# A mixture-of-experts block in front of a second mixer: output shares added in another order, router rows kept in natural order, a key norm moved up, and empty expert rows skipped by the gathers' bound

## The reference, cut to what matters

```python
# first block
x = x + diff_attention(rmsnorm(x, norm_mix), ...)
h = rmsnorm(x, norm_ffn)
logit_g = h @ w_group + b_group                 # 4 groups
logit_e = h @ w_router + b_router               # 16 experts
# each token: the best group, in it the best two of four experts, two weights
x = x + sum over the two experts of weight * (silu(h @ w_gate[e]) * (h @ w_up[e])) @ w_down[e]
# second block
xn = rmsnorm(x, norm_g) * (1 + sc_x) + sh_x
f_in, f_gate, q, k, v, na_gate = split(xn @ w_in)
q, k = rmsnorm(heads(q)), rmsnorm(heads(k))     # likewise keys and values of 256 context rows
mix = concat(fourier(f_in) * silu(f_gate), neighbourhood_attention(q, k, v, ...) * silu(na_gate))
x = x + g_x * (mix @ w_out)
```

## Time and profile before

| | us |
|---|---|
| median of 3 runs | 910.46 (909.38 to 911.85) |
| profiled execution, whole time | 911.67 |
| its span in the trace | 909.9 |
| PE busy | 890.8 (98%) |
| DVE, ACT, POOL busy | 377.2, 214.8, 177.5 |

### The profile page before, as it was taken

One profiled execution on the slowest core, in us unless ns is written; L12 is line 12 of the kernel. 1 busy time (PEld: TensorE's weight loads), 2 busy tenths in 40 slices (PEclk: granted clock), 3 DMA queues, 4 the chain that ended last, 5 costly groups with the idle time before them and its releaser, 6 DMA issues.

```text
span 909.9 us, 13423 instructions
## 1 busy us (share of the span) xinstructions
PE 890.8 (98%) x5562; PEld 505.1 (56%) x5562; DVE 377.2 (41%) x810; ACT 214.8 (24%) x469; POOL 177.5 (20%) x164
## 2 busy tenths in 40 slices
PE   9999999999999989999999999999999999999997
PEld 5588875455564433333333333344688888856553
DVE  2765442457755453310310210047635542454355
ACT  2211213345544210010110110124201111633320
POOL 3211220000003054230320200033202203290001
PEclk9999999999999999999999999999999999999999
DMA  9945559024011978999999999961382102700002
GB/s 326 322 112 186 185 207 390 29 93 185 1 47 52 277 197 329 412 415 426 423 422 428 421 429 428 402 234 47 110 173 100 42 15 79 246 1 2 1 1 92
DMA packets 71470, 188.47 MB, mean 207 GB/s; under 512 B 31201, under 2 KB 31857, under 8 KB 65137
## 3 DMA queue, kind: packets, MB, share of 16 engines
q1 hardware_dynamic: 62432, 162.41, 48.7%
q0 software_dynamic: 5488, 18.37, 5.4%
q10 hardware_dynamic: 3488, 6.82, 2.0%
HBM read 168.70 MB, written 18.89 MB: 206 GB/s over the span
## 4 chain that ended last, share of the span: by engine, by line
PE 81%; DMA 7%; DVE 5%; ACT 2%; POOL 2%; issue 2%; SPq 0%; DVEq 0%; ACTq 0%; POOLq 0%
PE psum L974 20%; PE psum L1178 14%; PE psum L1199 8%; PE psum L882 6%; PE psum L1076 5%; DMA ring<-in_moe_w_up 5%; PE psum L1024 4%; PE psum L1001 4%; PE psum L1329 2%; PE psum L1038 2%; PE psum L1055 2%; PE psum L1449 2%; PE psum L1398 2%; PE psum L1103 2%; PE psum L1291 2%
## 5 line engine op out<-in xcount | busy, mean ns | idle before, releaser
L1178 PE MATMUL psum<-ring,buf_a 128*32 128x512 f32 x1536 | 168.5, 597 | 3.8 <-issue 2.8
L1178 PEld LDWEIGHTS psum<-ring,buf_a 128*32 128x32 f32 x1536 | 53.5, 111 | 115.2 <-issue 115.2
L1199 PE MATMUL psum<-ring,buf_c 128*32 128x512 f32 x768 | 84.1, 593 | 0.0
L2712 POOL DMA_INDIRECT buf_b<-xq_d,o_sb x48 | 51.6, 1075 | 158.2 <-DVE buf_a L2296 126.1
L2319 DVE TENSOR_TENSOR buf_c<-buf_c,psum 128x512 f32<-128x512 f32 x12 | 13.1, 1089 | 154.4 <-PE psum L1178 154.4
L2639 POOL TENSOR_TENSOR qk_st<-qk_st,half 128x8 f32<-128x8 f32 x26 | 43.6, 1677 | 158.6 <-DVE qk_st L2378 72.9
L974 PE MATMUL psum<-ring,buf_a 128*128 128x256 f32 x320 | 70.9, 380 | 0.0
L974 PE MATMUL psum<-ring,buf_b 128*128 128x256 f32 x288 | 64.8, 380 | 0.0
L974 PEld LDWEIGHTS psum<-ring,buf_a 128*128 128x128 f32 x320 | 60.1, 190 | 8.2 <-issue 0.4
L1946 DVE TENSOR_TENSOR s_buf<-s_buf,psum 128x512 f32<-128x512 f32 x52 | 35.3, 685 | 61.2 <-PE psum L974 57.3
L974 PEld LDWEIGHTS psum<-ring,buf_b 128*128 128x128 f32 x288 | 53.9, 190 | 7.5 <-issue 0.6
(11 more groups left out here) (322 smaller groups left out, 1239.2 us busy)
## 6 DMA issues: line engine op xcount, KB each, us to landing
ring<-in_moe_w_gate SPq DMA_DIRECT2D x16, 2048.0 KB, 15.1
ring<-in_moe_w_up SPq DMA_DIRECT2D x16, 2048.0 KB, 16.0
ring<-in_moe_w_down SPq DMA_DIRECT2D x16, 2048.0 KB, 15.4
ring<-in_w_in SPq DMA_DIRECT2D x7, 2048.0 KB, 14.3
ring<-in_w_ada SPq DMA_DIRECT2D x6, 2048.0 KB, 9.7
ring<-in_da_w_in SPq DMA_DIRECT2D x5, 2048.0 KB, 15.8
y_d<-ring POOLq DMA_DIRECT2D x1, 5632.0 KB, 22.2
y_d<-buf_b ACTq DMA_DIRECT2D x11, 512.0 KB, 12.2
```

The costliest lines, as they stand in the source:

```text
L1178: last = mm(buf("mm", n)[rows, :], x_part[:, j, k, :], slot(moe_load(q, m, r))[:, k, :], start=(k == 0), stop=(k == KD - 1))
L1199: last = mm(buf("sc", n)[rows, m, :], hidT[:, s % 3, f * P + SUB * j:f * P + SUB * (j + 1)], slot(moe_load(q, 2, r), FC)[:, f, m * CH:(m + ...
L2712: pool.indirect_dma_start(out=xg[:, s % 2, j * 256:(j + 1) * 256], out_offset=None, in_=xn_quarters, in_offset=bass.IndirectOffsetOnAxis(a ...
```

## The change

- `xs2` is written in the order of `x`; PE's transposes read every eighth column of it, and `x_turn` reads the gathered rows so. `xn_d` and its four stores are gone; `xq_d` is stored with one DMA for a tile, those of the first three tiles ahead of SP's load of the sixth matrix.
- The token numbers in `slot_pick` are lowered by 4096 and 4*4096 is added back in `quarter`, so that a slot without a token has an index beyond the table. The gathers are given a bound, beyond which a row is not fetched.
- The places of tokens beyond 96 (`spill_places`) are worked out later, with the `picks` step among the experts' steps.
- The first key norm, j=CT, is moved ahead of the last tile's third norm on DVE and POOL, in parts.
- The output shares: every product is added straight from PSUM to each quarter of `x` that it belongs to (13 additions of a quarter and two of half a quarter, all on DVE, none on ACT or POOL); the order of the products and of the stores is another, and one mix sum is made earlier.

```diff
+NO_ROW = 8 * SEQ
+    out_bank |= {"P3": out_bank["P1"], "P7": out_bank["P5"], "P6": out_bank["P2"]}
@@ SP
+        def store_rows(t):
+            sp.wait_ge(xs2_ready, t + 1)
+            sp.dma_start(xq_d[t * P:(t + 1) * P, :], xs2[:, t, :]).then_inc(xq_stored, 16)
         for i in [0, 1, 4, 2, 5, 3, *range(SLOTS, len(order))]:
...
             elif i == 3:
-                for t in range(TT):
-                    sp.wait_ge(xs2_ready, t + 1)
-                    for n in range(4):
-                        sp.dma_start(xq_d[t * P:(t + 1) * P, n * 256:(n + 1) * 256].rearrange("p (k a) -> p k a", k=KD),
-                                     xs2[:, t, :].rearrange("p (k q a) -> p k q a", k=KD, q=4)[:, :, n, :]
-                                     ).then_inc(xq_stored, 16)
+                store_rows(TT - 1)
                 filled(sp, "sc", turn["sc", "cv"])
...
             load(moe_load(q, m, r), matrix(m, 4 * q + r), FC if m == 2 else KD)
+            if i == 2:
+                for t in range(TT - 1):
+                    store_rows(t)
...
-        for ready, t, a in ((1, 0, 0), (1, 1, 0), (2, 2, 0), (2, 3, 0), (0, 2, 1), (0, 3, 1), (3, 0, 1), (4, 1, 1)):
+        for added, t, a in ((5, 0, 0), (5, 1, 0), (11, 2, 0), (11, 3, 0), (12, 2, 1), (12, 3, 1), (13, 0, 1), (13, 1, 1)):
+            sp.wait_ge(out_added, added)
+            if added == 13:
+                sp.wait_ge(out_ready, t + 1)
@@ PE
+        def xs2_rows(t, k):
+            return xs2[:, t, :].rearrange("p (q k) -> p k q", k=KD)[:, k]
-                        transposes(n, [xs2[:, t, k * P:(k + 1) * P] for t in range(TT - 1)])
+                        transposes(n, [xs2_rows(t, k) for t in range(TT - 1)])
...
         out_seventh("S3", "T3", out_bank["P5"])
-        pe.wait_ge(s_out_ready, 2)
+        pe.wait_ge(s_out_ready, 3)
+        pe.wait_ge(out_added, 4)
+        out_seventh("S2", "T2", out_bank["P3"])
+        pe.wait_ge(out_added, 7)
+        out_seventh("A22", "T4", out_bank["P7"])
         out_seventh("S1", "T1", out_bank["P4"])
...
         pe.wait_ge(s_out_ready, 4)
-        pe.wait_ge(out_added, 6)
-        out_seventh("S4", "B22", out_bank["P4"])
+        out_seventh("S4", "B22", out_bank["P6"])
@@ DVE
+        link(V.tensor_scalar(quarter[:], quarter[:], 4.0 * NO_ROW, None, ALU.add))
-                V.tensor_scalar(xs2[:, t, :].rearrange("p (k q) -> p q k", k=KD),
-                                x[:, t, :].rearrange("p (q k) -> p q k", k=KD),
-                                rstd[:, 4 + t:5 + t], None, ALU.mult).then_inc(xs2_ready, 1)
+                V.tensor_scalar(xs2[:, t, :], x[:, t, :], rstd[:, 4 + t:5 + t], None, ALU.mult).then_inc(xs2_ready, 1)
-                            tok_f[:, t:t + 1], ALU.is_equal, ALU.mult).then_inc(pick_ready, 1)
+                            tok_below[:, t:t + 1], ALU.is_equal, ALU.mult).then_inc(pick_ready, 1)
-            V.transpose(xsT[:, s % 4, :], xg[:, s % 2, :]).then_inc(x_turned, 1)
+            V.transpose(xsT[:, s % 4, :].rearrange("p (j k a) -> p j k a", j=4, k=KD),
+                        xg[:, s % 2, :].rearrange("p (j a k) -> p j k a", j=4, k=KD)).then_inc(x_turned, 1)
             elif name == "picks":
+                spill_places()
                 last_picks()
...
         add_last(3)
-        norm3_mean(3)
-        norm3(3)
         for t in range(TT):
...
             qk_mean(CT + t)
+            if t == 0:
+                norm3_mean(3)
             qk_scale_unit(CT + t)
+            if t == 0:
+                norm3(3)
...
+        dve.wait_ge(mix_ready, TT)
+        mix_sum(3)
         add_out_f(turn["sc", "out_f", TT - 1], TT - 1)
-        dve.wait_ge(mix_ready, TT)
-        for n in (3, 1, 2, 4):
+        for n in (1, 2, 4):
             mix_sum(n)
...
# the additions in their new order, waits left out:
# x11 x12 x21 x22 of P1; x11 of P2; x21 x22 of P5; x21 x22 x12 of P3;
# x21 of P7; x22 x12 of P4; then the two halves of x12 of P6
@@ POOL
-            for t in tiles:
-                pool.wait_ge(xs2_ready, t + 1)
-                pool.dma_start(xn_d[t * P:(t + 1) * P, :], xs2[:, t, :]).then_inc(xn_stored, 16)
-        pool.wait_ge(xn_stored, TT * 16)
...
-                                        in_offset=bass.IndirectOffsetOnAxis(ap=idx[:, 4 * s + j:4 * s + j + 1], axis=0)
+                                        in_offset=bass.IndirectOffsetOnAxis(ap=idx[:, 4 * s + j:4 * s + j + 1], axis=0),
+                                        bounds_check=4 * SEQ - 1, oob_is_err=False
...
         norm3_power(2)
+        qk_power(CT)
         norm3_power(3)
...
-        pool.wait_ge(u2_ready, 1)
-        pool.wait_ge(out_added, 5)
-        G.tensor_tensor(x_part["x22"], x_part["x22"], out_u2, ALU.add).then_inc(x22_added, 1)
```

More of the change, by code:

```diff
@@ L401, in build @@
     t_out = [ring[:, 2, n * 1024:(n + 1) * 1024].rearrange("p (k n) -> p k n", k=2) for n in range(4)]
-    out_u2, out_p1 = (buf_d[:, n * 1024:(n + 1) * 1024].rearrange("p (a n) -> p a n", a=2) for n in (2, 3))
     s_out = [buf_d[:, n * 512:(n + 1) * 512].rearrange("p (k n) -> p k n", k=2) for n in range(4)]
@@ L1127, in _ @@
             claim(pe, "tp", n)
-            transposes(n, [xs2[:, TT - 1, k * P:(k + 1) * P] for k in range(4 * b, 4 * b + 4)])
+            transposes(n, [xs2_rows(TT - 1, k) for k in range(4 * b, 4 * b + 4)])
         router_three(6, KD)
@@ L1234, in _ @@
                     for g in range(KD):
-                        last = transpose(TP[g // 4][:, g % 4 * P:(g % 4 + 1) * P], xg[:, 0, g * P:(g + 1) * P], ident[:])
+                        rows = xg[:, 0, :].rearrange("p (q k) -> p k q", k=KD)[:, g]
+                        last = transpose(TP[g // 4][:, g % 4 * P:(g % 4 + 1) * P], rows, ident[:])
                     last.then_inc(spill_pe, 1)
@@ L1840, in _ @@
                         drain(S.copy(probs_T[m % 2][:, hh, :], buf("tp", n)), "tp", n)
-        act.wait_ge(out_added, 1)
-        S.copy(out_p1, out_bank["P1"]).then_inc(p1_out_copied, 1)
     @block.vector
@@ L2240, in _ @@
               "mm", n)
-        length = place[:, TT, :]
-        tiles, upto = full_tiles[:, 0, :], full_tiles[:, 1, :]
-        link(V.tensor_scalar(tiles, length, float(CAP), None, ALU.is_gt))
-        for q in (1, 2, 3):
-            link(V.scalar_tensor_tensor(out=tiles, in0=length, scalar=float(CAP + q * P), in1=tiles,
-                                        op0=ALU.is_gt, op1=ALU.add))
-        link(V.tensor_tensor_scan(upto, ones[:, 0:16], tiles, 0.0, ALU.mult, ALU.add))
-        before = s_buf[:, 0, 0, 0:SPILL * EXPERTS].rearrange("p (o e) -> p o e", o=SPILL)
@@ L2250, in _ @@
-        spill_f = s_buf[:, 0, 1, 0:SPILL + 1]
-        link(V.tensor_tensor(before, upto.unsqueeze(1).to_broadcast([P, SPILL, EXPERTS]),
-                             iota16[:, 0:SPILL].unsqueeze(2).to_broadcast([P, SPILL, EXPERTS]), ALU.is_le))
-        V.tensor_reduce(spill_f[:, 0:SPILL], before, AX.X, ALU.add)
-        link(V.tensor_copy(spill_f[:, SPILL:SPILL + 1], upto[:, EXPERTS - 1:EXPERTS]))
-        link(V.tensor_scalar(spill_f, spill_f, float(EXPERTS - 1), None, ALU.min))
-        V.tensor_copy(spill_i[:], spill_f).then_inc(spill_ready, 1)
@@ L2258, in _ @@
-        spill_base, step_back = full_tiles[:, 2, :], full_tiles[:, 3, :]
-        link(V.tensor_tensor(spill_base, upto, tiles, ALU.subtract))
-        link(V.tensor_scalar(spill_base, spill_base, float(P), float(SETS * P - CAP), ALU.mult, ALU.add))
-        link(V.tensor_tensor(step_back, row_96[:], spill_base, ALU.subtract))
-        link(V.tensor_scalar(r_a[:], place[:, 0:TT, :], float(CAP), None, ALU.is_lt))
-        link(V.tensor_tensor(r_a[:], r_a[:], step_back.unsqueeze(1).to_broadcast([P, TT, EXPERTS]), ALU.mult))
@@ L2529, in mix_sum, with add_out @@
             V.tensor_tensor(mix_part[f"S{n}"], mix_part[left], mix_part[right], op).then_inc(s_out_ready, 1)
-        def add_out(part_of_x, bank):
-            rows = x_part[part_of_x]
-            return V.tensor_tensor(rows, rows, out_bank[bank], ALU.add)
+        def add_out(part, product):
+            rows = x_part[part]
+            V.tensor_tensor(rows, rows, out_bank[product], ALU.add).then_inc(out_added, 1)
         for s in range(MIXER_STEPS):
@@ L2613, in _ @@
             rows = x_part["x12"][:, a, :]
-            V.tensor_tensor(rows, rows, out_bank["P4"][:, a, :], ALU.add).then_inc(out_ready, 1)
+            V.tensor_tensor(rows, rows, out_bank["P6"][:, a, :], ALU.add).then_inc(out_ready, 1)
     @block.gpsimd
@@ L2770, in bias_table @@
                             rel[:, :, :, shift:shift + KC], ALU.subtract).then_inc(bias_ready, 1)
-        for j in range(CT, len(QK2)):
+        for j in range(CT + 1, len(QK2)):
             qk_power(j)
```

105 lines of the change are left out of this document (59 added, 46 removed).

## The result

The changed kernel takes 901.15 us (median of 4 runs, 901.05 to 901.64). The kernel before took 911.15 us beside it (median of 4, 909.38 to 914.66). The ratio is 0.9894, with a 95% interval of 0.9867 to 0.992. The profiled execution of the changed kernel took 901.18 us with a span of 899.4, against 911.67 and 909.9 before, so the two traces can be set against each other directly: 10.5 us.

What follows compares the result with a forecast made beforehand. PE, busy 890.8 of 909.9 us, was taken as the bound, so only its waits and the tail could be won: router 1.5, experts 1.1, key norm 1.6, end 2.0, together 6.2, from 910.46 to 904.3 us; range 901.5 to 908.0.

Steps and rivals of the forecast that it cites:

- The router's sum: Before the first gate product: 2.76 us gained with 0.6 of waiting left, less 1.3 for strided loads, giving 1.5.
- the term for weight loads with steps: Router: PE's 32 transposed blocks reading with 32-byte steps cost 0.04 us more each, 1.3 us in all.
- The rival of 3.2 us: Router: strided weight loads are dear on PE, 3.2 us instead of 1.3, giving 906.2; chance 0.16.
- DVE's 0.2 and 0.8 for its steps: Router: x_turn's strided reads cost 0.2 us once in the first set, 0.8 us in each other set, hidden beside PE.
- 1.46 for 1.1: Expert stage: the gathers' bound spares 2.1 MB and removes PE's waits for expert matrices, gain 1.1 us.
- The rival that the transfer is not spared: Expert stage: rows beyond the bound still cost their transfer, the 1.1 us of waits stay, 905.4; chance 0.08.
- 2.04 for 1.6: First key norm: moved earlier, it removes PE's wait for the first key tile, gain 1.6 us.
- 2.93 for 2.0: Kernel's end: DVE keeps up and the last store is issued about 904.5 instead of 906.5, gain 2.0 us.
- that rival: Kernel's end: DVE's additions slip beyond the 0.8 us margin and PE waits; two slips of 0.7 give 905.7; chance 0.07.
- P5's two: Kernel's end: two DVE additions from 890.1 to 892.5, wanted by PE at 893.3, the smallest margin, 0.8 us.
- The rival of the dearer gather: POOL before the first gate product: a bounded gather takes 1.8 us, four cost 3.4 more, 907.7; chance 0.06.
- the slower case at 2.8 us a gather: POOL's queue after idx: gathers at 2.8 us each use up the 6.2 gain, slower by 0.3% from 3.5; chance 0.05.

Runs made afterwards that it cites:

- the router alone: Kernel before with only plain rows of xs2, early whole-row stores, strided weight loads and transposes, and later spill_places, without the gathers' bound: 908.86 us (0.9977).
- the key norm's kernel: Kernel before with only the first key norm moved ahead of the third norm of t=3: 908.11 us (0.9967).
- the two whose ten extra products run 250 us earlier: Ten unread products of 128 columns added behind the router's last products: 911.62 us (1.0024) in the kernel before, 903.7 us (0.9913) in the changed kernel.

## Why the prediction was too careful

Two steps failed. The router's sum priced TensorE's wait by its length alone and put at nothing what it did to the clock of the products behind it: 1.70 us. And the term for weight loads with steps, 1.3 us, measured under 0.1. The range's lower end had room for free steps and for 0.9 us behind the last store, both of which came, but not for the clock.

**Router, stores and gathers.** The mechanism was right. Without a price for steps and without the bound's delay it gave 2.76 us with 0.6 of waiting left; the router alone gave 2.94 with 0.65. In the whole change 1.99 came, since the first gather starts 0.62 later and the four gathers come 1.30 apart instead of 1.25. The prediction had taken a gather with a bound at the old 0.95 from start to end and did not ask where its start lies. The edit that writes the bound once gives 0.65 of it back.

**Router, the price of steps.** Mis-sized: 1.3 us in the sum, under 0.1 measured. The reasoning from the column price of a load failed at "if the step doubles this": the load does get 50 ns longer, but lies beside the product before it. The rival of 3.2 us had 0.16 and is refuted. DVE's 0.2 and 0.8 for its steps were right, and hidden as said. There was some luck in it: L2319, from which they were taken, steps by four floats in PSUM as well as in SBUF, so it did not show what SBUF's steps alone cost.

**Router, the clock.** Missing, 1.70 us, the largest single error. The forecast subtracted waits and took the work behind them as fixed. The profile of before had the evidence: the first 156 products take 18.64 us, 119 ns each, where 64 undisturbed ones take 7.00, 109 each. The wait filled in the kernel before shows the cause.

**Experts.** 1.46 for 1.1. The waits went as forecast, and 2.1 MB were spared. The rival that the transfer is not spared is refuted. But the sentence that an earlier start "isn't lost to DMA" holds only because of the bound: without it 2.4 of the router's 4.6 us are lost again by the end of the stage, and the bound is worth 3.8 us at that point (2.5 in the medians). In stage times the parts don't add: the router alone has 2.22 of its 4.64 left at the second block. In the medians they do, within their noise: 1.5, 3.1, 2.3 and 2.8 give 9.7 of the 10.0.

**Key norm.** 2.04 for 1.6, and no new wait. **The end.** 2.93 for 2.0. The forecast put the start of the last store's issue 2.0 earlier; counted from the seven products it is 1.9 (906.5 and 897.0). The rest, 1.0, is what lies behind that start, 3.4 us before and 2.4 after, which the forecast had left as it was: the issue itself is shorter (it ends at 907.17 and 897.34), and from that end to the span's end it is 2.06 instead of 2.73. No addition was late, so that rival is refuted. P5's two, with the smallest margin, ended at 884.87, 0.9 ahead of the product that wants them (885.75; 0.8 forecast).

**One pattern.** A wait of TensorE was worth some tenths of a us more than it showed: 1.05 in two waits gave 1.46 in the experts, 1.64 gave 2.0 at the key norm, and the router alone lost 3.88 in that stage to 3.47 of waits. Of this 0.17 a wait is the counting shown at the key norm's kernel; the rest is open. The rival of the dearer gather, and the slower case at 2.8 us a gather, are refuted with 1.00 us and a pace of 1.30.

Together: 6.2, plus 1.3 for steps, less 0.8 for the gathers' start and pace, plus 1.7 for the clock, 0.4, 0.4 and 0.9 for experts, key norm and end, 0.4 for a stretch with nothing in it, gives 10.5.

## What to carry to other kernels

A wait is worth its length only if the clock behind it stays: set the time of the same group of products behind the wait against that of an undisturbed group, and read the granted clock there, before pricing its removal. Where compute and transfers are level, an edit that saves bytes and one that starts the compute earlier have to be priced together: without the saved bytes, more than half of the earlier start was lost again in waits (4.64 us ahead, 2.22 left). When an operation gets an operand held in a register, look at which instruction carries the wait: writing the register once, ahead of the wait, gave back 0.65 us at the first gate product, 0.4 of them at the end.

## What was not expected of the hardware

**The clock and the length of a wait.** Behind waits up to 1.69 us the 320 products lasted 34.54; behind 2.69, 2.76, 4.28 and 8.52 they lasted 36.04, 36.24, 36.93 and 36.60. But in the expert stage a wait of 2.33 us left the clock up and one of 1.99 us let it fall to 0.51, so length alone doesn't decide. (Behind 2.83 us it stood at 0.50.) The Trainium skill's page "TensorE: Matmul & The Clock Gate", section "Part 1: The HAM clock gate (the "warmup" mystery)", says that the clock follows TensorE's recent activity and is watched on a schedule of its own, so that the same kernel can come out differently; the two waits fit that, and no run here tests it.

**A store that lands later beside ten extra products.** The last store into `y_d` released POOL after 6.91 to 7.05 us in twelve kernels with the same code there, whenever it was issued, and after 8.23 and 8.30 in the two whose ten extra products run 250 us earlier. There it cost TensorE 1.3 and 1.6 us. The cause is open.

**Steps in weight loads.** 141 ns plain, 193 with 32-byte steps, 211 with 16-byte steps, for 128 columns of float32; only the 16-byte steps lengthened a group of 32 transposes, by 0.3 to 0.4 us.
